# A sample-attention stage: value pages are issued by ScalarE on its own queue instead of by SyncE

## The chip, the cores and the metric

The kernel runs as one program on one core of a Trainium2 chip. The metric is device time in microseconds (us), from one launch to its end; lower is better.

## The reference

The kernel is one inference step of a two-layer decoder trunk (a convolution layer, then an attention layer, each followed by a mixture of experts). The change lies in the attention layer, in the part that serves the eight sample sequences. Each has 4 new tokens and 512 past positions whose keys and values lie in a paged pool, 4 pages of 128 positions for each sequence, found by a page table:

```python
k_past = cache_k[page_table].reshape(B, past, N_HEADS, HEAD_DIM)   # B = 8, past = 512
v_past = cache_v[page_table].reshape(B, past, N_HEADS, HEAD_DIM)   # 16 heads of 64
z = jnp.einsum('bqhd,bkhd->bhqk', q, k) * (HEAD_DIM ** -0.5) + bias
log_fail = jnp.where(mask, jax.nn.log_sigmoid(-z), 0.0)
between = lax.cumsum(log_fail, axis=3, reverse=True) - log_fail
attn = jnp.where(mask, jnp.exp(jax.nn.log_sigmoid(z) + between), 0.0)
o = jnp.einsum('bhqk,bkhd->bqhd', attn, v)
```

A page of keys or of values is 128 positions by 1024 features in float32, 512 KB. The stage reads 32 key pages and 32 value pages.

## The kernel before

The program is a row of stages; each stage is one block in which every engine has its own instruction stream, and the streams meet only at semaphores and at the stage's end. The stage here is `stage_sample_attention`. It takes the sequences in four pairs, p = 0 to 3. Both sequences of a pair share the 128 rows of a score tile (2 sequences, 16 heads, 4 tokens).

For each pair TensorE does these steps in this order:

- `keys_turned`: the pair's key pages are transposed in 16 chunks (m = 0 to 7 from the first sequence's pages, 8 to 15 from the second's), through three PSUM banks; after each chunk semaphore `t` goes up. The copies out of PSUM (`keys_out`) are shared between ScalarE (semaphore `ka`) and VectorE (`kd`). For the first pair ScalarE takes the odd chunks, for later pairs chunks 2, 3, 4, 5, 7, 9, 11, 13 and 15 (`by_act`). Chunk i can be turned only when chunk i-3 has been copied.
- `scores`: it waits until all 16 copies of the pair are done, by both engines, and multiplies queries by keys (L657, L661). VectorE and ScalarE then work out the weights (L810 to L825, with ScalarE's Exp, Ln, Exp at L740, L742, L746).
- `weights_turned` (L670, L671): the weights are transposed; ScalarE copies them out (L752, L753).
- `values` (L684, L686): it waits for the copied weights and for the pair's eight value pages, multiplies, and raises `av`.
- `pick` (L693): after VectorE's `own_features` (L783) the wanted heads are gathered.

The next pair's `keys_turned` is laid between these steps by hand: chunks 0 to 9 after `scores`, 10 to 13 after `weights_turned`, and 14 and 15 after `values`. So chunk 15 of the next pair, which ScalarE copies, comes after the values of this one and ahead of the next scores.

Pages come in through `load_pages` (L428 to L435), a hardware loop over 4 pages: a register is loaded from the page table, checked, and a DMA issued with it. In the kernel before, SyncE alone runs it. For every pair its stream first issues the next pair's key pages (4 pages when chunk 7 of this pair has been turned, 4 when chunk 15 has), and then the eight value pages of this pair, which from the second pair on wait for `av` of the pair before, since there is one buffer for each of the two sequences.

Of the kernel before, what the change touches and what calls it, by code (L numbers as in the profile page):

```python
# [427 lines left out]
def load_pages(K, sp, seq, base, name, sem):  # L428

    pages = K.region(base, NPG, D)  # L430
    npool = K.d["cache_k"].shape[1]
    src = K.d["cache_" + name][0].rearrange("n r h c -> n r (h c)")
    with sp.Fori(seq * NPG, seq * NPG + NPG) as g:
        page = sp.value_load(K.ptab[0:1, bass.ds(g, 1)], min_val=0, max_val=npool - 1)
        sp.dma_start(pages[:, bass.ds(g - seq * NPG, 1), :].rearrange("p a c -> p (a c)"), src[page]).then_inc(sem, 16)  # L435
# [105 lines left out]
def stage_sample_attention(K):  # L541
# [6 lines left out]
    s = {n: K.sem(f"sample_{n}") for n in names}  # L548
# [38 lines left out]
    NCH = 2 * KT  # L587
# [15 lines left out]
    with nc.Block() as block:  # L603
        @block.sync
        def _(sp):
            load_pages(K, sp, 1, K.keys_in[1], "k", K.s_keys[1])
            for p in range(PAIRS):
                for u in range(2):
                    if p < PAIRS - 1:
                        sp.wait_ge(s["t"], NCH * p + KT * (u + 1))  # L610
                        load_pages(K, sp, 2 * p + 2 + u, K.keys_in[u], "k", K.s_keys[u])
                for u in range(2):
                    if p > 0:
                        sp.wait_ge(s["av"], p)
                    load_pages(K, sp, 2 * p + u, K.values_in[u], "v", K.s_values[u])

        @block.gpsimd
        def _(pool):
# [98 lines left out]
        def keys_out(eng, copy, on_act, p, first, last):  # L717

            for m in range(first, last):
                i = NCH * p + m  # L720
                if by_act(i) == on_act:
                    u, k = divmod(m, KT)
                    if p > 0:
                        eng.wait_ge(s["z"], p)
                    eng.wait_ge(s["t"], i + 1)
                    copy(KS[u][:, k, :], K.ps[TB[i % 3]][:]).then_inc(s["ka" if on_act else "kd"], 1)

        @block.scalar
        def _(act):
            a = nc.scalar  # L730
            a.preload_act_table_set("natural_log_exp_and_others")

            def keys(p, first, last):
                keys_out(act, lambda o, i: a.activation(o, i, ACT.Copy), True, p, first, last)

            keys(0, 0, NCH)
            for p in range(PAIRS):
                more = p + 1 < PAIRS
                act.wait_ge(s["c"], p + 1)
                a.activation(lo, lo, ACT.Exp).then_inc(s["e"], 1)  # L740
                act.wait_ge(s["e"], p + 1)
                a.activation(lo, lo, ACT.Ln, bias=1.0).then_inc(s["l"], 1)  # L742
                if more:
                    keys(p + 1, 0, 6)
                act.wait_ge(s["tt"], p + 1)
                a.activation(A, A, ACT.Exp).then_inc(s["ea"], 1)  # L746
                if more:
                    keys(p + 1, 6, 8)
                act.wait_ge(s["atr"], p + 1)
                if p > 0:  # L750
                    act.wait_ge(s["av"], p)
                a.activation(AT[:, 0:NPG, :], K.ps[7].rearrange("p (g r) -> p g r", r=P), ACT.Copy)  # L752
                a.activation(AT[0:NS, NPG, :], ATn, ACT.Copy).then_inc(s["at"], 1)  # L753
                if more:
                    keys(p + 1, 8, NCH)

        @block.vector
        def _(dve):
# [1351 lines left out]
```

## Time and profile before

| | us |
|---|---|
| median of 3 runs | 1451.08 |
| lowest and highest run | 1450.27, 1457.32 |
| the profiled execution's own time | 1453.72 |
| its span, first to last instruction | 1451.9 |
| the stage of the change in it (824.9 to 958.0) | 133.1 |
| mean granted TensorE clock, as a share of full | 0.907 |

Times in the rows are counted from the span's start. PE is TensorE's matmul (a transpose is one too), PEld its weight load, DVE VectorE, ACT ScalarE, POOL GpSimd, SP SyncE; a q behind a name (SPq, ACTq) is that engine's instruction sequencer, which issues DMAs and runs register and branch instructions. In a timeline the bracket says how long the engine had been idle before the row and whose end released it.

### The profile page before, as it was taken

The page shows a single profiled execution, that of the slowest core. Times are in us where ns is not written, and L with a number is a line of the kernel's source. Part 1 is how long each engine was busy: PE and PEld are TensorE (multiplying, and loading weights), DVE is VectorE, ACT ScalarE, POOL GpSimd, SP SyncE. Part 2 cuts the span into 40 slices and gives each one's busy share as a digit, 9 for nine tenths or more (in the row PEclk, how much of TensorE's full clock was granted, in tenths as well). Part 3 has the DMA queues.
Part 4 walks back from the last instruction along what each step waited for, and adds up shares of the span by engine and source line. Part 5 has one row for each costly group of instructions (what it writes and reads, how often), then busy time and mean ns, then how long its engine had stood idle before and what let it go on. Part 6 is the DMA issues. An engine that isn't in the chain of part 4 may idle for free. (4 is left out here: it accounts for less than half of the span.)

```text
span 1451.9 us, 15639 instructions
## 1 busy us (share of the span) xinstructions
PE 1174.0 (81%) x5862; PEld 675.8 (47%) x5862; DVE 528.5 (36%) x959; ACT 264.8 (18%) x482; POOL 126.8 (9%) x206
## 2 busy tenths in 40 slices
PE   3999997959988877289999566589999699888870
PEld 3866753533333332168888543345545333333320
DVE  2499994142322221400000333346731433222215
ACT  3101125220000000300000222236632200000001
POOL 0300010011111110000000100012310111111100
PEclk9999998978999999579999889879999889999995
DMA  8222206056999994332223587660043569999955
GB/s 219 38 58 73 102 1 267 34 208 254 423 425 425 426 425 200 130 93 69 71 72 101 181 290 251 233 201 5 0 168 127 208 243 421 425 424 425 425 213 208
DMA packets 110330, 310.77 MB, mean 214 GB/s; under 512 B 22290, under 2 KB 65042, under 8 KB 85672
## 3 DMA queue, kind: packets, MB, share of 16 engines
q1 hardware_dynamic: 99750, 287.41, 51.8%
q0 software_dynamic: 9216, 17.85, 3.3%
q10 hardware_dynamic: 1298, 4.62, 0.8%
q8 instruction: 43, 0.70, 0.2%
q14 instruction: 23, 0.19, 0.0%
HBM read 295.56 MB, written 29.02 MB: 224 GB/s over the span
## 5 line engine op out<-in xcount | busy, mean ns | idle before, releaser
L1706 PE MATMUL psum<-arena 128*64 128x512 f32 x1024 | 258.8, 663 | 61.1 <-DMA arena<-moe_w_up 58.3
L1706 PEld LDWEIGHTS psum<-arena 128*64 128x64 f32 x1024 | 88.8, 152 | 228.8 <-issue 225.2
L476 PE MATMUL psum<-arena 128*128 128x272 f32 x768 | 179.2, 397 | 6.1 <-DMA arena<-sb_w_qkv 6.1
L476 PEld LDWEIGHTS psum<-arena 128*128 128x128 f32 x768 | 147.8, 193 | 37.5 <-issue 6.4
L1994 DVE TENSOR_TENSOR arena<-arena,psum 128x256 f32<-128x256 f32 x32 | 13.5, 421 | 308.3 <-ACT arena L1895 308.3
L1720 PE MATMUL psum<-arena 128*64 128x512 f32 x512 | 116.9, 598 | 8.4 <-DVE arena L1998 8.4
L1299 PE MATMUL psum<-arena 128*128 128x272 f32 x512 | 121.4, 398 | 1.6 <-DVE arena L1496 1.0
L1548 DVE SCALAR_TENSOR_TENSOR arena<-arena,vec 128x512 f32<-128x512 f32 x169 | 113.3, 743 | 0.0
L1299 PEld LDWEIGHTS psum<-arena 128*128 128x128 f32 x512 | 98.0, 193 | 23.6 <-issue 2.9
L499 DVE TENSOR_SCALAR arena<-psum 128x272 f32 x24 | 10.6, 441 | 174.8 <-PE psum L476 174.8
L1895 ACT ACTIVATE arena<-psum 128x256 f32<-128x256 f32 x32 | 12.3, 383 | 323.1 <-PE psum L1706 323.1
L1737 POOL DMA_INDIRECT rows_out<-arena x32 | 32.2, 1006 | 432.8 <-DVE arena L2008 422.4
L1720 PEld LDWEIGHTS psum<-arena 128*64 128x64 f32 x512 | 33.9, 136 | 66.8 <-issue 54.8
L1381 PE MATMUL psum<-arena 128*128 128x512 f32 x128 | 58.5, 612 | 3.3 <-ACT arena L1452 3.3
L1057 PE MATMUL psum<-arena 128*128 128x512 f32 x128 | 56.4, 595 | 2.0 <-PEq L143 2.0
L1313 PE MATMUL psum<-arena 128*128 128x512 f32 x126 | 55.5, 593 | 0.0
L1899 ACT ACTIVATE arena<-psum 128x512 f32<-128x512 f32 x32 | 19.1, 597 | 167.4 <-PE psum L1720 167.4
L1004 POOL TENSOR_SCALAR_AFFINE_SELECT arena<-arena 128x128 f32<-128x128 f32 (+1 forms) x96 | 31.1, 349 | 208.7 <-DVE arena L990 189.7
L1725 DVE TENSOR_TENSOR arena<-count,arena 128x1280 bf16<-128x1280 f32 x32 | 47.2, 1482 | 0.1
L1699 PEld LDWEIGHTS psum<-ident,arena 128*128 128x128 f32 x256 | 31.9, 193 | 30.2 <-issue 24.3
L643 PE MATMUL psum<-ident,arena 128*128 128x128 f32 x256 | 37.2, 298 | 8.8 <-DMA arena<-cache_k 5.6
L684 PE MATMUL psum<-arena 128*32 128x512 f32 x128 | 20.5, 799 | 28.2 <-DMA arena<-cache_v 28.2
(261 smaller groups left out, 1283.5 us busy)
## 6 DMA issues: line engine op xcount, KB each, us to landing
arena<-moe_w_gate SPq DMA_DIRECT2D x64, 1024.0 KB, 18.4
arena<-moe_w_up SPq DMA_DIRECT2D x64, 1024.0 KB, 24.3
arena<-moe_w_down SPq DMA_DIRECT2D x64, 1024.0 KB, 24.0
arena<-cache_k SPq DMA_DIRECT2D x32, 512.0 KB, 4.7
arena<-cache_v SPq DMA_DIRECT2D x32, 512.0 KB, 4.8
arena<-sb_w_qkv SPq DMA_DIRECT2D x24, 512.0 KB, 3.5
arena<-conv_w_pw SPq DMA_DIRECT2D x16, 512.0 KB, 5.2
arena<-rows_out SPq DMA_DIRECT2D x16, 512.0 KB, 6.5
```

The source lines that it names most:

```text
L476: last = nc.tensor.matmul(K.ps[2 * u + n][:, 0:HALF], wt[u][:, k, :], HT[:, k, n * HALF:(n + 1) * HALF], start=(k == 0), stop=(k == KT - 1))
L643: last_t = nc.tensor.transpose(K.ps[TB[i % 3]][:, g * P:(g + 1) * P], kp[u][:, g, k * P:(k + 1) * P], K.ident[:])
L1057: last = nc.tensor.matmul(K.ps[4 + i % 4][:], OT[:, k, b * P:(b + 1) * P], K.wo[:, k, n * 512:(n + 1) * 512], start=(k == 0), stop=(k == K ...
L1299: last = mm(K.ps[2 * h + n][:, 0:HALF], K.c_w[ct % 3][:, k, h, :], HT[:, k, n * HALF:(n + 1) * HALF], start=(k == 0), stop=(k == KT - 1))
L1313: last = mm(taps(ct)[:], diag[ct % 2][:, j, :], stream(ct, j), start=(j == 0), stop=(j == n - 1))
L1381: last = mm(K.ps[4 + i % 4][:], C[:, k, b, 0:P], K.w2[:, k, n * 512:(n + 1) * 512], start=(k == 0), stop=(k == KT - 1))
L1548: last = v.scalar_tensor_tensor(out=y, in0=x, scalar=wj, in1=y, op0=ALU.mult, op1=ALU.add)
L1699: last = nc.tensor.transpose(xt_ps[:, k, :], xr[:, k::KT], K.ident[:])
L1706: last = mm(out[half[q], :].rearrange("t (m f) -> t m f", m=2), xe[:, k, half[q]], wgu[u][:, :, k, :], start=(k == 0), stop=(k == KT - 1))
L1720: last = mm(K.ps[4 + n][half[q], :], hT[:, j, half[q]], wd[u][:, j, n * 512:(n + 1) * 512], start=(j == 0), stop=(j == NJ - 1))
L1725: return nc.vector.tensor_tensor(oh, K.count[:].unsqueeze(1).to_broadcast([P, 2 * NB, P]), places.unsqueeze(2).to_broadcast([P, 2 * NB, P] ...
L1737: return nc.gpsimd.indirect_dma_start(K.y_dram, bass.IndirectOffsetOnAxis(ap=idx[:, g, 1:2], axis=0), y, None, bounds_check=2 * TOK - 1, o ...
```

## The change

SyncE no longer issues value pages. ScalarE does: the first pair's eight pages at the beginning of its stream, right behind the loading of its function table, and the pages of pair p + 1 when the values of pair p have been multiplied (`av`), between its copies of chunk 13 and of chunk 15. SyncE keeps the key pages, with the waits that they had. Nothing changes in what is computed, in the buffers, or in TensorE's, VectorE's and GpSimd's streams.

```diff
@@ SyncE @@
                     if p < PAIRS - 1:
                         sp.wait_ge(s["t"], NCH * p + KT * (u + 1))
                         load_pages(K, sp, 2 * p + 2 + u, K.keys_in[u], "k", K.s_keys[u])
-                for u in range(2):
-                    if p > 0:
-                        sp.wait_ge(s["av"], p)
-                    load_pages(K, sp, 2 * p + u, K.values_in[u], "v", K.s_values[u])
@@ ScalarE @@
+            for u in range(2):
+                load_pages(K, act, u, K.values_in[u], "v", K.s_values[u])
             keys(0, 0, NCH)
...
                 if more:
-                    keys(p + 1, 8, NCH)
+                    keys(p + 1, 8, 14)
+                    act.wait_ge(s["av"], p + 1)
+                    for u in range(2):
+                        load_pages(K, act, 2 * p + 2 + u, K.values_in[u], "v", K.s_values[u])
+                    keys(p + 1, 14, NCH)
```

## Rows read from the trace of the kernel before

**Rows 1.** TensorE's waits in the stage: waiter, releaser, us in total, times, longest.
```profile
...
PE psum L684 <- DMA arena<-cache_v: 28.2, 4, 8.8
...
PE psum L643 <- DMA arena<-cache_k: 5.6, 4, 1.9
```

**Rows 2.** Timeline, second pair to last: start us, us, engine, line, operation, [idle, releaser].
```profile
...
870.67 0.69 DVE L783 TENSOR_TENSOR arena<-psum,arena 128x512 f32<-128x512 f32 x1 [13.03 <-PE psum L686]
...
871.72 0.60 ACT L734 ACTIVATE arena<-psum 128x512 f32<-128x512 f32 x1 [13.53 <-PE psum L643]
...
872.42 3.64 PE L657 MATMUL psum<-arena 128*32 128x512 f32 x32
...
895.50 4.92 PE L684 MATMUL psum<-arena 128*32 128x512 f32 x32 [8.80 <-DMA arena<-cache_v]
...
901.48 0.69 DVE L783 TENSOR_TENSOR arena<-psum,arena 128x512 f32<-128x512 f32 x1 [14.41 <-PE psum L686]
...
925.54 5.25 PE L684 MATMUL psum<-arena 128*32 128x512 f32 x32 [8.24 <-DMA arena<-cache_v]
...
931.85 0.69 DVE L783 TENSOR_TENSOR arena<-psum,arena 128x512 f32<-128x512 f32 x1 [14.19 <-PE psum L686]
...
945.75 0.25 ACT L753 ACTIVATE arena<-psum 32x128 f32<-32x128 f32 x1
...
949.23 5.36 PE L684 MATMUL psum<-arena 128*32 128x512 f32 x32 [4.01 <-DMA arena<-cache_v]
...
955.64 0.69 DVE L783 TENSOR_TENSOR arena<-psum,arena 128x512 f32<-128x512 f32 x1 [12.50 <-PE psum L686]
```

**Rows 3.** Timeline, the stage's start and the first pair, all engines.
```profile
...
824.95 1.28 ACT L731 ACT_TABLE_LOAD   x1 [9.78 <-PEq L503]
...
831.51 0.60 ACT L734 ACTIVATE arena<-psum 128x512 f32<-128x512 f32 x1 [5.28 <-PE psum L643]
...
840.54 3.64 PE L657 MATMUL psum<-arena 128*32 128x512 f32 x32 [0.73 <-ACT arena L734]
...
852.32 1.22 PE L643 MATMUL psum<-ident,arena 128*128 128x128 f32 x8 [1.84 <-DMA arena<-cache_k]
...
856.63 0.86 PE L643 MATMUL psum<-ident,arena 128*128 128x128 f32 x4
...
864.61 5.00 PE L684 MATMUL psum<-arena 128*32 128x512 f32 x32 [7.11 <-DMA arena<-cache_v]
```

**Rows 4.** Timeline of SyncE's queue: first issue, us to the last one's end, pages.
```profile
...
836.20 11.34 SPq L435 DMA_DIRECT2D arena<-cache_k  x8
...
885.64 5.91 SPq L435 DMA_DIRECT2D arena<-cache_v  x4
...
932.84 11.37 SPq L435 DMA_DIRECT2D arena<-cache_v  x8
```

**Rows 5.** Sequencer instructions by line: ns min/median/max, first and last start.
```profile
...
L1676 ACTq TENSOR_LOAD <-over x2: 297/384/472, 578.0 to 1413.0; - x2
...
L1676 SPq TENSOR_LOAD <-over x2: 282/382/482, 578.0 to 1413.0; - x2
...
L224 ACTq DMA_DIRECT2D rows_in<-arena x10: 333/337/374, 255.0 to 1145.4; - x10
...
L435 SPq DMA_DIRECT2D arena<-cache_v x32: 342/345/351, 848.7 to 943.9; - x32
```

**Rows 6.** Clock: weight loads in time; windows with us, busy, clock, DMA, GB/s.
```profile
...
896.33 0.22 PEld L684 LDWEIGHTS psum<-arena 128*32 128x32 f32 x4 [0.62 <-issue]
...
898.51 0.14 PEld L684 LDWEIGHTS psum<-arena 128*32 128x32 f32 x4 [0.29 <-issue]
...
880.70:882.60 1.90, 0.02 (x1) 1.00 0.97 334
...
891.00:895.50 4.50, 0.00 (x0) 0.53 0.87 250
...
949.20:952.60 3.40, 3.37 (x16) 0.91 (x20) 0.00 (x0) 0.00 (x0) 0.00 (x0) 0.50 0.02 5
```

## The prediction, made before the changed kernel ran

> **What bounds the kernel now.** I read the page first, then TensorE's waits inside the stage, then the timeline pair by pair, then SyncE's queue, and last the clock. A row of the page's chain that ended last says nothing here: it is four microseconds of the final stage, since all engines meet between stages. So the stage is judged by TensorE, whose stream has every step of a pair in it. The waits show where it stands still: 28.2 us in four waits for value pages, 5.6 us for key pages, and both hang on one queue [rows 1]. The timeline gives the beat. VectorE's L783 starts as the values of a pair end; it starts at 870.67, 901.48, 931.85 and 955.64, so the pairs take 30.8, 30.4 and 23.8 us [rows 2]. In the second and third pair TensorE stood ready 8.80 and 8.24 us before the pages were in, in the last one 4.01, in the first one 7.11 [rows 2, 3].
>
> The reason is issue, not transfer. Eight pages take SyncE 11.37 us from the first issue to the end of the last [rows 4]; the last issue itself is 0.345 [rows 5], so one page costs (11.37 - 0.345) / 7 = 1.575 us of a sequencer: register load, checks, branch and DMA. Sixteen pages are 25 us of each pair, with waits between them. The change halves SyncE's load. The question is who pays for the other half.
>
> **What it takes away.** All four waits for values should go: the first pair's pages are issued at the stage's beginning, the others right behind `av`, some 15 us before they are wanted (below). The last pair gets only 3.2 us of its 4.01, because the weights are not copied before 945.75 + 0.25 = 946.0 and the values began at 949.23 [rows 2]. Key pages no longer queue behind value pages; of the 5.6 us [rows 1] I credit 0.5 us in each of pairs 2 and 3 (bounds 0 and the longest such wait, 1.9), since the weights are due at about the same time as the keys.
>
> **What it adds, per pair.** ScalarE issues pages at its sequencer, in order, and behind them in its stream stands its copy of chunk 15. TensorE's next scores wait for that copy, VectorE and ScalarE's logarithms wait for the scores. Nothing covers this: before, the copy at 871.72 came 1.05 us after L783's start, and the scores 0.70 behind it, 1.75 in all [rows 2]. Does ScalarE's sequencer do a page faster than SyncE's? No row shows the loop on it. But its register load from memory (297 to 472 ns) stands beside SyncE's in the same line (282 to 482), and its DMA issue is 337 against 345 ns [rows 5]. I take SyncE's 1.575 us; bounds are the DMA issue alone, 0.34, and SyncE's slowest stretch, (5.91 - 0.35) / 3 = 1.85 [rows 4, 5]. Then, counted from L783's start T: release to first issue 0.99 (931.85 to 932.84), eight pages 11.37 [rows 2, 4], about 0.1 for the loop's end, copy to scores 0.70. The scores start at T + 13.2 instead of T + 1.75: +11.4 us in pairs 2, 3 and 4.
>
> The Trainium skill speaks against that price. In "DMA: Bandwidth & Descriptors", section "Issuing engines are not separate DMA queues", it says that DMAs of several engines run on the same 16 DMA engines and that issuing from more than one saves only sequencer time, "which is usually small relative to the DMA itself". By that sentence ScalarE would hardly be held, and the time would be that of the second rival. The trace disagrees for this loop.
>
> **The clock.** After a long pause TensorE is at the lower level of its clock: in the wait before 895.50 the granted clock fell (mean 0.53 from 891.00 to 895.50), and a group of four weight loads with the gap before it took 0.22 + 0.62 = 0.84 us, later 0.14 + 0.29 = 0.43 [rows 6]. About three groups run slow, 1.3 us. A short pause did not do it (1.00 from 880.70 to 882.60 [rows 6]). The change moves the long pause from before the values to before the scores: +1.3 on the scores of pairs 2 to 4 (bounds 0 and 3.4, all eight groups slow), -1.3 on the values of pairs 1 to 3. The last pair's values ran at 0.50 [rows 6], and as nothing busy stands ahead of them there, they stay so.
>
> **The first pair.** ScalarE's eight pages begin about 1 us into the stage, or behind the table load of 1.28 us that starts at 824.95 [rows 3]: first issue at 825.9 or 827.2; I take 826.6, so it is free at about 826.6 + 11.4 + 0.1 = 838.1. Its first copy was at 831.51 [rows 3]; TensorE turns four chunks and then waits for it, as the bank of chunk 1 is wanted for chunk 4. With the copy done at 838.7, chunks 4 to 7 at 0.86 us for a cold one [rows 3] (three cold, one at about 0.5) end at 841.9. SyncE's next eight key pages wait for chunk 7: first issue 0.99 later, 842.9 instead of 836.20 [rows 4], +6.7. TensorE took up chunk 8 of the next pair when these were in, at 852.32 [rows 3]; now 859.0. The scores, moved from 840.54 [rows 3] by some 6 us, are not what ends last there, as the keys come 12 us after them. From 852.32 to the end of chunk 13 (856.63 + 0.86 = 857.49) it took 5.2 us, so the values start at 864.2 against 864.61 [rows 3]. The 7.11 us that the early pages save are paid back by late keys: -0.4, and -1.3 for the clock, -1.7.
>
> **The sum.** First pair -1.7. Second: 11.4 + 1.3 - 0.5 - 8.8 - 1.3 = +2.1. Third: 11.4 + 1.3 - 0.5 - 8.2 - 1.3 = +2.7. Fourth: 11.4 + 1.3 - 3.2 = +9.5; there SyncE was nearly free before, and ScalarE's issue is pure loss. Total +12.6 us. TensorE's pages wait disappears and a larger one, for ScalarE, takes its place. The stage's end moves with it, and nothing behind it depends on which queue issued. The profiled span of 1451.9 would be 1464.5; that execution's own time was 1453.72, 1.8 around the span, and is 2.6 above the median 1451.08, to which I add: 1463.7 us, +0.87%. A change of under 0.5% (7.3 us) can't be told from none here.
>
> **Where it turns.** A page's price counts 7 times in the first pair and 7 in each of three others, 28 times. The sum is zero at 1.575 - 12.6 / 28 = 1.13 us a page; it is +7.3 at 1.39 and -7.3 at 0.86.
>
> **Rivals.**
> - A dearer page (chance 0.13). If ScalarE's loop runs at SyncE's slowest pace, 1.85 us [rows 4], 28 times 0.28 adds 7.8 us: 1471.5. Two streams at once could do the like by contention: the DMA engines were already 0.97 busy at 334 GB/s from 880.70 to 882.60 [rows 6]. Eight value and four key pages (6.29 MB) at that rate are 19 us, from T + 1 to T + 20. The values are wanted at about T + 28 (8.80 us before 895.50 TensorE was ready, 14.3 us after the scores began [rows 2], and these now begin at T + 13.2 with 1.3 lost), the second half of the keys at about T + 24. That fits, so I don't count it; keys 2 us late in each pair would end near 1469.
> - Faster: ScalarE is barely held (0.05). If its register work runs ahead, and only the 0.34 us of the DMA issue [rows 5] count, eight pages hold it for 2.7 us. The scores start at T + 4.4, the pairs from the second on change by about -7.5, -7 and -0.5, the first gains up to 7 (ScalarE is free before its first copy is due): some -22 us, 1429. For it speaks that the gain of the waits is real; against it that SyncE's own register work is not hidden and ScalarE's instructions cost the same [rows 5].
> - About even (0.07): a page at 1.13 to 1.39 us on ScalarE, 1451 to 1458. It takes a loop a fifth cheaper than SyncE's, which no row shows.
>
> The forecast has 0.75. Its own range, from a scores step that stays at the full clock (-3.9), pages 5% off (2.2) and the first pair's 1.3 us of doubt, is 1458 to 1470. The range given is 1456 to 1471. Slower by over 0.5% holds the forecast, a small end of it aside, and the dearer page: 0.86; within 0.5% 0.09; faster 0.05.
>
> **What the profile would show.** The waits of L684 for value pages are gone. In their place L657 waits for ScalarE's L734, three times about 11 us. Value pages are issued on ScalarE's queue 1.55 to 1.6 us apart, beginning near 826 and then 1 us behind each `av`. ScalarE's first copy is near 838, the key pages of the second pair begin near 843, the first values near 864. L783 comes about 32 us apart, the last time 33. L657's mean rises from the full clock's, L684's falls. I am wrong if the pages on ScalarE's queue are much closer than 1.4 us, if its copies run in between, or if TensorE then waits for keys at the second half of a pair.

## The result and the profile after

The changed kernel takes 1463.73 us (median of 5 runs, 1457.99 to 1468.27). Against runs of the kernel before the ratio is 1.0068, 95% interval 1.0045 to 1.0092: slower by 0.68%, some 9.9 us. The forecast was 1463.7 us, +0.87%, from a sum of 12.6 us; the interval holds it. That the two times agree to 0.1 us is luck: the forecast was laid on a median of 1451.08, and the runs of the kernel before that stand beside the experiments have medians of 1453.2 to 1454.0.

The profiled execution spans 1462.3 us, 10.4 more than before. The stage itself shows the change more sharply. It goes from ScalarE's table load at 824.79 to its next one at 971.26, 146.5 us against 133.1 (824.95 to 958.07 before), so +13.4. What lies behind the stage took 491.0 us here and 493.8 before; over all the executions in this study it lay between 490.8 and 493.8, and the stage began between 822.3 and 828.5. So up to 6 us ahead of the stage and 3 us behind it are scatter in any difference between two spans, and the experiments below are read by the stage. A stage time is that of one execution, though, and a ratio comes from four to eleven. For the change the ratio's 9.9 us (6.5 to 13.4) lie below the stage's 13.4, and in most of the other versions it is so too, by 1.4 to 6.0 us: stage times within some 3 us of each other are not told apart here.

TensorE's waits in the stage after the change (waiter, releaser, us in total, times, longest; line numbers have moved by four for the copies and the two products, so that L653 is the scores, L680 the values, L639 the turning of keys, L730 ScalarE's copy of a chunk, L751 its copy of turned weights, L785 what was L783):

```profile
PE psum L653 <- issue: 32.7, 3, 11.5
...
PE psum L639 <- ACT arena L730: 5.3, 4, 4.0
...
PE psum L639 <- DMA arena<-cache_k: 1.6, 1, 1.6
PE psum L680 <- ACT arena L751: 0.8, 1, 0.8
```

The 28.2 us of waits for value pages [rows 1] have gone, all four. In their place stand three waits of the scores, 32.7 us. "Issue" only says that the profile found no releaser; the timeline names it. From the second pair on:

```profile
866.02 0.69 DVE L785 TENSOR_TENSOR arena<-psum,arena 128x512 f32<-128x512 f32 x1 [4.27 <-PE psum L682]
...
866.93 11.44 ACTq L435 DMA_DIRECT2D arena<-cache_v  x8
...
878.62 0.60 ACT L730 ACTIVATE arena<-psum 128x512 f32<-128x512 f32 x1 [16.53 <-issue]
879.31 6.11 PE L653 MATMUL psum<-arena 128*32 128x512 f32 x32 [11.48 <-issue]
...
895.79 3.64 PE L680 MATMUL psum<-arena 128*32 128x512 f32 x32
...
900.49 0.69 DVE L785 TENSOR_TENSOR arena<-psum,arena 128x512 f32<-128x512 f32 x1 [4.27 <-PE psum L682]
...
912.91 6.38 PE L653 MATMUL psum<-arena 128*32 128x512 f32 x32 [10.61 <-issue]
...
934.35 0.69 DVE L785 TENSOR_TENSOR arena<-psum,arena 128x512 f32<-128x512 f32 x1 [4.27 <-PE psum L682]
...
946.74 6.53 PE L653 MATMUL psum<-arena 128*32 128x512 f32 x32 [10.58 <-issue]
...
962.09 5.69 PE L680 MATMUL psum<-arena 128*32 128x512 f32 x32 [0.83 <-ACT arena L751]
...
968.83 0.69 DVE L785 TENSOR_TENSOR arena<-psum,arena 128x512 f32<-128x512 f32 x1 [9.65 <-PE psum L682]
```

Read it as one chain. The values of the first pair end at 866.02. ScalarE's queue issues eight pages until 878.37 (866.93 + 11.44). A quarter of a microsecond later ScalarE makes its one copy, and 0.69 us behind the copy's start the scores begin, 13.29 us after L785's start instead of 1.75 [rows 2]. The values then follow without a wait and run at the full clock in 3.64 us instead of 4.92 [rows 2]. The pairs after the first take 34.5, 33.9 and 34.5 us, against 30.8, 30.4 and 23.8.

The stage's beginning in the timeline:

```profile
824.79 1.28 ACT L727 ACT_TABLE_LOAD   x1 [9.73 <-PEq L503]
...
825.73 10.46 ACTq L435 DMA_DIRECT2D arena<-cache_v  x8
...
836.37 1.09 ACT L730 ACTIVATE arena<-psum 128x512 f32<-128x512 f32 x2 [10.29 <-issue]
...
857.00 1.45 PE L639 MATMUL psum<-ident,arena 128*128 128x128 f32 x8 [1.61 <-DMA arena<-cache_k]
...
861.33 3.64 PE L680 MATMUL psum<-arena 128*32 128x512 f32 x32
```

ScalarE's first copy moves from 831.51 to 836.37, SyncE's next key pages from 836.20 to 841.43 (the row below, from the timeline of its queue), chunk 8 of the second pair from 852.32 to 857.00, and the first values start at 861.33 instead of 864.61 [rows 3, 4].

```profile
841.43 5.08 SPq L435 DMA_DIRECT2D arena<-cache_k  x4
```

What a page costs ScalarE's sequencer, by line (ns min/median/max):

```profile
L434 ACTq TENSOR_LOAD <-ptab x32: 277/282/297, 825.0 to 944.7; - x32
...
L435 ACTq DMA_DIRECT2D arena<-cache_v x32: 353/358/407, 825.7 to 945.4; - x32
```

The spacing is (10.46 - 0.36) / 7 = 1.44 us for the first pair's pages and (11.44 - 0.36) / 7 = 1.58 for the second's; the issues that begin at 901.39 and 935.26 take 10.58 and 10.54 us, 1.46 a page.

The clock before and during the scores of the second pair, in two views (windows with us, busy time of the engines, clock, DMA share, GB/s; then weight loads in time):

```profile
868.00:878.50 10.50, 0.00 (x0) 0.00 (x0) 0.16 (x2) 0.00 (x0) 0.00 (x0) 0.63 0.89 322
879.30:882.80 3.50, 3.49 (x20) 0.99 (x24) 0.00 (x0) 0.00 (x0) 0.00 (x0) 0.50 1.03 420
```

```profile
883.55 0.23 PEld L653 LDWEIGHTS psum<-arena 128*32 128x32 f32 x4 [0.63 <-issue]
884.38 0.14 PEld L653 LDWEIGHTS psum<-arena 128*32 128x32 f32 x4 [0.60 <-issue]
884.81 0.14 PEld L657 LDWEIGHTS psum<-arena 128*32 128x32 f32 x4 [0.29 <-issue]
```

With TensorE idle since about 868 the granted clock fell to half (0.50), the 1.2 GHz level, and six groups of weight loads came 0.86 us apart before the 0.43 us of the full clock returned; in the values of before it had been three [rows 6]. The scores took 6.11, 6.38 and 6.53 us against 3.64.

### The profile page after: what moved, and what is told of

It reads as the page before. It is cut to its first block and busy times, and to the rows that moved or that the text cites. A ratio compares the mean times of both kernels' runs of the same rounds, so it can differ in the third digit from the quotient of the medians.

```text
span 1462.3 us, 15642 instructions
## 1 busy us (share of the span) xinstructions
PE 1178.2 (81%) x5862; PEld 676.6 (46%) x5862; DVE 529.5 (36%) x959; ACT 264.6 (18%) x483; POOL 126.6 (9%) x206
## 5 line engine op out<-in xcount | busy, mean ns | idle before, releaser
L499 DVE TENSOR_SCALAR arena<-psum 128x272 f32 x24 | 10.6, 442 | 174.9 <-PE psum L476 174.9
L1722 PEld LDWEIGHTS psum<-arena 128*64 128x64 f32 x512 | 33.9, 136 | 66.8 <-issue 54.8
L653 PE MATMUL psum<-arena 128*32 128x512 f32 x128 | 22.7, 872 | 33.4 <-issue 32.7
L639 PE MATMUL psum<-ident,arena 128*128 128x128 f32 x256 | 37.2, 297 | 12.8 <-ACT arena L730 5.3
```

The costliest lines, as they stand in the source:

```text
L639: last_t = nc.tensor.transpose(K.ps[TB[i % 3]][:, g * P:(g + 1) * P], kp[u][:, g, k * P:(k + 1) * P], K.ident[:])
L1722: last = mm(K.ps[4 + n][half[q], :], hT[:, j, half[q]], wd[u][:, j, n * 512:(n + 1) * 512], start=(j == 0), stop=(j == NJ - 1))
```

## The experiments

The theory under test is that ScalarE's sequencer is held by the issue of eight pages, 11 to 12 us, and that its copy of chunk 15, on which the scores wait, stands behind. The rivals are transfers of two queues that slow each other, and the clock. In the table a pair's time is the distance between the starts of VectorE's multiplication behind the values (L783 before); the first pair's is counted from the table load that opens the stage, and the stage runs to the table load that ends it.

| run | ratio to before (95%) | stage us | pairs 1 to 4, us |
|---|---|---|---|
| before | | 133.1 | 45.7, 30.8, 30.4, 23.8 |
| the change | 1.0068 (1.0045 to 1.0092) | 146.5 | 41.2, 34.5, 33.9, 34.5 |
| e1_first_only | 0.9961 (0.9946 to 0.9976) | 131.8 | 41.5, 30.6, 32.9, 24.4 |
| e2_later_only | 1.0111 (1.0086 to 1.0136) | 149.2 | 44.8, 33.7, 33.9, 34.5 |
| e3_copy15_dve | 0.9927 (0.9904 to 0.9951) | 122.3 | 41.4, 26.2, 26.4, 25.9 |
| e4_pool | 0.9949 (0.9929 to 0.9968) | 129.1 | 42.2, 33.3, 26.7, 24.5 |
| e5_fixed_pages | 0.9901 (0.9876 to 0.9926) | 124.7 | 40.9, 26.5, 27.8, 27.1 |
| e7_read_ahead | 0.9901 (0.9880 to 0.9922) | 121.7 | 41.5, 27.5, 28.1, 22.2 |
| e8_pool_half | 0.9866 (0.9843 to 0.9890) | 115.5 | 39.0, 26.0, 25.2, 22.9 |
| e9_sp_known | 0.9884 (0.9860 to 0.9908) | 118.7 | 41.3, 27.1, 27.1, 20.8 |
| e10_both_known | 0.9905 (0.9885 to 0.9925) | 120.7 | 40.0, 31.6, 24.5, 22.2 |

### e1: the first pair alone, and e2: the later pairs alone

```diff
 # both against the change
 # e1, SyncE (ScalarE: the first pair's pages only)
+                if p > 0:
+                    sp.wait_ge(s["av"], p)
+                    for u in range(2):
+                        load_pages(K, sp, 2 * p + u, K.values_in[u], "v", K.s_values[u])
 # e2, SyncE (ScalarE: the later pairs' pages only)
+                if p == 0:
+                    for u in range(2):
+                        load_pages(K, sp, u, K.values_in[u], "v", K.s_values[u])
```

> The first pair alone: ScalarE issues its value pages at the stage's beginning, SyncE those of pairs 2 to 4 as in the kernel before. Theory (sequencer hold): the first pair ends 41.2 us after the stage's beginning as with the whole change (45.7 before), the others take 30.8, 30.4 and 23.8 us as before, the stage 128.6 us (133.1 before), the program 0.3% less. Rival (the early pages' gain is paid back by later waits): the stage stays at 133.

> Later pairs alone: SyncE issues the first pair's value pages as in the kernel before, ScalarE issues those of pairs 2 to 4. Theory (ScalarE's sequencer is held by the issue, ahead of its copy of chunk 15): the first pair ends as before, near 870.7, and the three others cost what they cost in the changed kernel, +3.7, +3.5 and +10.7 us; the stage takes about 151 us (133.1 before, 146.5 with the whole change) and the program 1.2% more than before. Rival (the two queues' transfers slow each other at the stage's beginning and leave everything late): without that beginning the stage falls below 146.5.

With the first pair alone it ended after 41.5 us, as with the whole change (41.2) and 4.2 us sooner than before. In the profiled execution 1.3 us of that gain was left at the stage's end, where 4.5 were expected: the third pair took 32.9 us instead of 30.4. There SyncE's value pages began at 910.02, 9.5 us after the multiplication's start at 900.57, instead of 8.3 (909.75 after 901.48); its four key pages ahead of them had taken 5.87 us instead of 5.08. What slows SyncE's loop in such stretches (it does so in the kernel before too [rows 4]) stayed open. As much again was the clock: the values of that pair took 6.41 us instead of 5.25. But this execution, 1453.52 us, is the slowest of the eleven runs of e1. Their median is 1448.48, and their ratio makes the program 5.7 us faster (3.5 to 7.8), as much as was expected; so the gain of the first pair lasts, and the loss in the third pair is not shown to be usual.

With the later pairs alone the first ended after 44.8 us, the others took 33.7, 33.9 and 34.5, and the stage 149.2: the loss of the change is in pairs 2 to 4 and is the same without the early pages. The rival's fall below 146.5 did not come.

### e3: chunk 15 copied by VectorE

```diff
-        return m % 2 == 1 if p == 0 else m in (2, 3, 4, 5, 7, 9, 11, 13, 15)
+        return m % 2 == 1 if p == 0 else m in (2, 3, 4, 5, 7, 9, 11, 13)
```

> The changed kernel, but chunk 15 of pairs 2 to 4 is copied by VectorE, so that no copy stands behind the issue of value pages in ScalarE's stream. Theory (hold): the scores start about 2.5 us after the values of the pair before, not 13.2; what then waits for ScalarE is its first Exp, which comes about 12.4 us after the values instead of 6.5, so pairs 2 to 4 take some 27 to 28 us instead of 34.5, 33.9 and 34.5; the stage takes about 126 us, below the 133.1 of before. Rivals (the lower clock, or transfers that slow each other, cost the time): the scores come early, but the stage stays within 3 us of 146.5.

One copy in a pair, moved from one engine to the other, takes 24 us out of the stage. Some 8 us of it is the clock: all three scores now run at the full clock, 3.64 us instead of 6.11, 6.38 and 6.53. Two rows of its timeline, second pair (the values of the first ended at 864.94):

```profile
867.11 3.64 PE L653 MATMUL psum<-arena 128*32 128x512 f32 x32 [0.36 <-DVE arena L722]
...
877.46 0.66 ACT L738 ACTIVATE arena<-arena 128x544 f32<-128x544 f32 x1 [16.45 <-issue]
```

The scores begin 2.2 us after the values and at the full clock, 3.64 us. The hold is still there, but ends later in the chain: ScalarE's Exp comes 12.5 us after the values, where the scores were ready at 871.1. The stage is at 122.3 against 126 expected; both rivals had it near 146. This version beats the kernel before.

### e4: GpSimd issues the value pages, and e8: half of each page

```diff
 # e4, GpSimd, behind its three mask operations; ScalarE as before the change, SyncE as in the change
+            for p in range(PAIRS):
+                if p > 0:
+                    pool.wait_ge(s["av"], p)
+                for u in range(2):
+                    load_pages(K, pool, 2 * p + u, K.values_in[u], "v", K.s_values[u])
 # e8, besides, in load_pages for values
-        sp.dma_start(pages[:, bass.ds(g - seq * NPG, 1), :]..., src[page])
+        sp.dma_start(pages[:, bass.ds(g - seq * NPG, 1), 0:D // 2]..., src[page][:, 0:D // 2])
```

> All value pages are issued by GpSimd, which has nothing else to do in the stage but three mask operations at its beginning; ScalarE and VectorE are as in the kernel before. Theory (hold): nothing on the path waits for the issue, so the gain of early pages comes without its price. At SyncE's 1.58 us a page the pages of a pair are in about 18.6 us after the values of the pair before and wanted after 16, so pairs 2 and 3 take some 24 us, the first ends near 861; the stage takes about 113 us, the program 1.4% less than before. The unknown is GpSimd's price: at about 2.4 us a page the pairs are as long as before. Rival (transfers of two queues slow each other): the waits for key pages grow and the stage does not fall below 133.

> As in the run with GpSimd's queue, but only the first half of each value page is loaded (256 KB instead of 512 KB, as many DMAs), which leaves out half of the values. Theory for the shortfall of that run (two queues share the transfer rate, and key pages come late): TensorE's waits for key pages fall from 15.7 us to under 5, those for value pages from 8.6 to under 3, the stage from 129.1 to about 114 us. Rival (GpSimd's issue itself is slow or late): the waits stay, and the stage with them within 3 us of 129.

GpSimd's price is SyncE's: 869.88 and 871.44 are two issues of its loop, 1.56 us apart. Nothing that is waited for stands behind them in GpSimd's stream, yet the stage fell only to 129.1 us, not to 113. The rival's growth of the waits for keys came (5.6 to 15.7 us), its bound of 133 did not. TensorE's waits in e4:

```profile
PE psum L644 <- DMA arena<-cache_k: 15.7, 3, 6.4
...
PE psum L685 <- DMA arena<-cache_v: 8.6, 2, 4.4
```

and in e8, with half the bytes of values and as many DMAs:

```profile
PE psum L647 <- DMA arena<-cache_k: 12.8, 3, 5.5
...
PE psum L688 <- DMA arena<-cache_v: 2.4, 1, 2.4
```

Half the bytes took 13.6 us off the stage (115.5), about as the sharing of the transfers asked (114), and the waits for values fell as expected. The waits for keys did not fall below 5 us: only a part of them went with the bytes. The rest may be SyncE's loop, which still needs 1.57 us a page for them (four in 5.05 us from 889.80) where a pair of 25 us wants its second half of keys sooner; no run here shows it apart.

### e5: fixed pages, no table read

```diff
+def load_fixed(K, eng, seq, base, name, sem):
+    pages = K.region(base, NPG, D)
+    src = K.d["cache_" + name][0].rearrange("n r h c -> n r (h c)")
+    for g in range(NPG):
+        eng.dma_start(pages[:, g, :], src[seq * NPG + g]).then_inc(sem, 16)
-                        load_pages(K, act, 2 * p + 2 + u, K.values_in[u], "v", K.s_values[u])
+                        load_fixed(K, act, 2 * p + 2 + u, K.values_in[u], "v", K.s_values[u])
 ... (the first pair's load likewise)
```

> The changed kernel, but ScalarE's value pages are fixed pages of the pool, issued in a row with no table read and no loop; this leaves out the look-up of value pages, so the values multiplied are those of other pages. Transfers are as many and as large. Theory (sequencer hold): a page costs ScalarE about 0.36 us, the copy of chunk 15 comes about 4 us after the values, pairs 2 to 4 take some 23 to 25 us and the stage about 111 us. Rival (transfers): pages that are issued closer together contend more, and the stage stays above 140. Rival (clock): the scores still run slow and the stage stays above 133.

The same bytes through the same queue, chunk 15 still behind them. Eight pages on ScalarE's queue now take

```profile
863.26 4.07 ACTq L442 DMA_DIRECT2D arena<-cache_v  x8
...
868.13 6.42 PE L660 MATMUL psum<-arena 128*32 128x512 f32 x32 [3.06 <-issue]
```

and the scores begin at 868.13, 4.9 us after the values instead of 13.3. The stage falls by 21.8 us to 124.7. It does not reach 111: the waits for keys grow from 1.6 to 10.3 us, and the scores still run cold (6.42, 5.13 and 6.60 us). The hold decides; late keys and the clock take back a part of what it gives. The pause before these scores was only 3.06 us, so a shorter hold did not bring the full clock back; e3, with 0.36 us, did.

### e7, e9 and e10: page numbers read ahead of the wait

```diff
+def page_numbers(K, eng, seq):
+    ...
+    return [eng.value_load(K.ptab[0:1, seq * NPG + g:seq * NPG + g + 1], ...) for g in range(NPG)]
+def load_known(K, eng, numbers, base, name, sem):
+    ... (pages and src as in load_fixed)
+    for g in range(NPG):
+        eng.dma_start(pages[:, g, :], src[numbers[g]]).then_inc(sem, 16)
 # e7, ScalarE (chunk 15 on VectorE as in e3)
+                    numbers = [page_numbers(K, act, 2 * p + 2 + u) for u in range(2)]
                     act.wait_ge(s["av"], p + 1)
                     for u in range(2):
-                        load_pages(K, act, 2 * p + 2 + u, K.values_in[u], "v", K.s_values[u])
+                        load_known(K, act, numbers[u], K.values_in[u], "v", K.s_values[u])
 # e9: SyncE issues all, keys and values, with numbers ahead of each wait (the stage's first keys excepted);
 #     ScalarE as before the change
 # e10: e7, SyncE's keys as in e9, and on ScalarE one more wait
+                    act.wait_ge(s["t"], NCH * (p + 2))
```

> Chunk 15 is copied by VectorE as in the run that moved that copy, and ScalarE reads the eight page numbers of the next pair into registers ahead of its wait for the values; behind the wait stand eight DMA issues and no loop. Theory (hold): at about 0.5 us a page ScalarE is free 5 us after the values, its Exp is wanted after 6.2, so nothing waits for the issue; pairs 2 to 4 then go by the transfers (eight value and four key pages at 330 to 350 GB/s are some 19 us) and take about 25 us, the stage about 117 us against 122.3, the program 1.1% less than before. Rival (transfers alone set the pace, the hold had been hidden): waits for pages take the place of the hold and the stage stays at 121 or above.

> SyncE issues everything, in the order of the kernel before, but reads the four page numbers of a group into registers ahead of the wait and then issues four DMAs with no loop (the first key group of the stage excepted). Theory (the price of a page on the sequencer is the cause, not the queue it stands on): at 0.4 to 0.5 us a page the waits for value pages fall from 28.2 us to under 12, the stage from 133.1 to about 118 us, the program about 1% less than before. Rival (a second queue is needed to feed the pages): the stage stays above 130.

> The two cheap issues together: SyncE issues key pages and ScalarE value pages, both with page numbers that are read ahead of the wait and with no loop (the stage's first key group and first pair of value pages excepted); chunk 15 is copied by VectorE, and ScalarE waits, beside the values, for chunk 15 to be turned, the event that lets SyncE issue the second half of the key pages. Theory (what was left with ScalarE's cheap issue were key pages that came late because eight value pages had been issued ahead of them): issued together, four key pages share the transfers with the first four value pages and are in some 12 us later, about when they are wanted; the waits for key pages fall from 15.8 us to under 6, the stage from 121.7 to about 115 us, below the 118.7 of SyncE alone. Rival (the transfers are full, and whatever is late only changes its name): waits for keys and values add up to 12 us or more and the stage stays at 118 or above.

In e7 the hold is gone: ScalarE's Exp at 871.13 follows the scores at once. What ends last now are keys, as two rows of its timeline show; below them is the window of that wait (us, busy time of the engines, clock, DMA share, GB/s):

```profile
864.37 4.18 ACTq L447 DMA_DIRECT2D arena<-cache_v  x8
...
881.61 1.97 PE L651 MATMUL psum<-ident,arena 128*128 128x128 f32 x8 [6.96 <-DMA arena<-cache_k]
```

```profile
874.70:881.60 6.90, 0.00 (x0) 0.00 (x0) 1.98 (x4) 1.14 (x2) 0.00 (x0) 0.79 1.03 419
```

The waits for key pages are 15.8 us, with the DMA engines full in the one shown: what the rival of that run said, that with the hold gone waits for pages take its place. Its bound does not decide, as the stage of 121.7 is too near its 121, and the ratio's 0.99% (0.78 to 1.20) holds the 1.1% of the theory.

In e9 no second queue is used at all, and the stage is at 118.7. Its waits:

```profile
PE psum L698 <- DMA arena<-cache_v: 14.6, 3, 5.6
...
PE psum L657 <- DMA arena<-cache_k: 1.1, 2, 0.5
```

28.2 us of waits for values became 14.6 (under 12 expected), with the same engine, the same order and the same waits. Four issues with known numbers took 1.93 us (from 872.16), 0.53 a page. So the stage gained without a second queue, and about half of the waits came from the register work between the issues. Most of the other half was transfer, as the windows of the three waits that were left show:

```profile
854.70:860.20 5.50, 0.00 (x0) 0.03 (x1) 0.29 (x1) 0.60 (x1) 0.00 (x0) 0.71 1.02 416
882.60:887.10 4.50, 0.00 (x0) 0.00 (x0) 0.27 (x1) 0.60 (x1) 0.00 (x0) 0.69 1.02 417
909.70:914.00 4.30, 0.00 (x0) 0.00 (x0) 0.29 (x1) 0.60 (x1) 0.00 (x0) 0.72 0.67 274
```

In the first two the DMA engines were full, at 416 and 417 GB/s; in the kernel before, the waits for the first and second pair's values show 344 and 285 GB/s (857.6 to 864.6, 886.8 to 895.4), at busy shares of 0.98 and 0.89: such a share did not mean that no more could be moved. In e10, with both queues cheap and keys and values released by the same event, the waits are

```profile
PE psum L652 <- DMA arena<-cache_k: 8.8, 3, 4.2
PE psum L693 <- DMA arena<-cache_v: 5.3, 1, 5.3
```

14.1 us together, and the stage is at 120.7 instead of 115: again the rival. The second pair lost most (31.6 us), the third, at 24.5, was the shortest third pair of all these runs. Of the versions that load the pages which the table asks for, e9 has the lowest ratio, 0.9884; its interval overlaps those of e7 and e10.

## Why the prediction was right, step by step

**The price and its place: right.** The waits for values went, three waits for chunk 15 of 10.6 to 11.5 us came, and e3 shows that this copy is the link: with it on VectorE the stage lost 24 us, all queues unchanged. e5 shows that the sequencer's price, not the bytes, makes the hold. A page on ScalarE's queue cost 1.44 to 1.58 us against the 1.575 taken from SyncE; the scores began at T + 13.3, + 12.4 and + 12.4 against T + 13.2.

**Issue, not transfer: half of it.** That sentence of the prediction does not follow from its rows: at the 334 GB/s of the window it quotes, a page of 512 KB takes 1.57 us to move, as long as its issue. The experiments part the two. With cheap issue on one queue (e9) 28.2 us of waits became 14.6, and in two of the three waits left the transfers were full. For the change itself it made no difference, as its hold is made of issue (e5).

**The first pair: mis-sized.** ScalarE's first issue is at 825.73, so its sequencer does not wait for the table load; I had taken the middle, 826.6. With 1.44 us a page its first copy came at 836.4 instead of 838.1, and the first pair gained 4.5 us (41.2 against 45.7) instead of 1.7. The values began at 861.33, 2.9 us ahead of the 864.2 foretold. Of that 1.7 is the earlier copy; chunk 8 came 15.6 us after the first key issue instead of 16.1; and from chunk 8 to the values it took 4.3 us instead of the 5.2 that had been carried over; the first key issue, 0.3 us later behind the copy than foretold, took a little back. These chunks had run at a mean clock of 0.67 before (852.3 to 857.5) and ran at 1.00 here (856.9 to 861.3), a term of the clock that the sum did not have. Its mechanism is as told: chunk 8 came 4.7 us later, which paid back most of the 7.11 us.

**The clock: right in kind, mis-sized.** I had taken three cold groups, 1.3 us, from the values of before. The scores lost 2.5, 2.7 and 2.9 us. In the second pair six groups ran at half clock instead of three; the bound of 3.4 held. What sets the number of slow groups stays open: it is not the length of the pause alone, since 11.48, 10.61 and 10.58 us cost 2.5, 2.7 and 2.9 here, and 3.06 us cost 2.8 in e5. That a short pause does not do it holds for the 1.9 us of the row quoted, and not for these 3.06. The values ran warm in pairs 1 to 3 (3.64 us), and in pair 4 cold as forecast.

**The sum.** Pairs 2 to 4 became longer by 3.7, 3.5 and 10.7 us against 2.1, 2.7 and 9.5. The clock added 1.2, 1.1 and 1.9 us over what was counted; in pairs 3 and 4 a hold that was 0.7 to 0.8 us shorter took a part back. With -4.5 for the first, the stage is 13.4 us longer, 12.6 forecast. That these lie so close is luck: two errors of some 3 us stand against each other. Two figures of the prediction do not follow from its own terms: the terms named for its own range give 1456.3 to 1467.2, not 1458 to 1470, and pairs of 32 us and a last one of 33 do not fit its sum, which gives 32.9, 33.1 and 33.3.

**The rivals.** The dearer page did not come. Contention did not show in this kernel (waits for keys 1.6 us, less than the 5.6 before), though value pages took 8.2 us to land instead of 4.8: nobody waited for them. That the hold gives the transfers time is argued from the runs without it (e4, e5, e7), where the waits for keys rose to 10 to 16 us. The faster rival, by the Trainium skill's sentence in "DMA: Bandwidth & Descriptors" ("Issuing engines are not separate DMA queues"), did not come either: sequencer time was not small beside the DMA here, 1.44 to 1.58 us a page where 512 KB at the 420 GB/s of the window from 879.30 to 882.80 take 1.25 (an estimate). The section's other half, that all queues run on the same 16 DMA engines and interleave, agrees with the late keys of e7 and the full DMA engines in that wait; the interleaving itself no run here shows.

## What to carry to other kernels

A DMA issue moved to a compute engine is paid for in that engine's stream: find the first instruction behind it that somebody waits for, and count issues times the sequencer's price up to there. Before a queue is split, look at what the price is made of; here reading table entries ahead of the wait did more on one queue (0.9884) than a second queue did with the loop kept (1.0068, or 0.9927 with the waiting copy out of the way, where the intervals just touch). When such a hold goes, look at once for what it was covering: here late key pages.

## What was not expected of the hardware

ScalarE's sequencer ran the page loop, table read and all, while ScalarE itself loaded its function table (first issue at 825.73, table load 824.79 to 826.07). GpSimd issued the same loop at 1.56 us a page, no dearer than SyncE. The number of slow groups of weight loads did not go by the pause before them: six after 11.5 us and three after the 8.8 us before the values, but in e5 the scores took 6.42 us, nearly twice 3.64, after 3.06 us.
